# Who makes the low parts of the second block's mixer weights, GpSimd or VectorE

## The reference, cut to what matters

```python
u = rmsnorm(h, mix_norm[l]) @ w_in[l]              # the input matrix: 24 tiles of 128 columns
qa, ka, va, qb, ckv, iq, ik, iw = jnp.split(u, IN_SPLITS_2, axis=-1)
...
o_a = diff_attention(qa, ka, va, lam, bias_a, a_subln[l], lam_init)
...
o_b = dsa_attention(q_lat, c, iq, ik, iw, b_w_uv[l], bias_b, topk)   # keys chosen by top-k of a score
h = h + jnp.concatenate([o_a, o_b], axis=-1) @ w_out[l]              # the output matrix
```

## The kernel before, in words

| piece | stands between | | piece | stands between |
|---|---|---|---|---|
| i0 | the last two sums of the feed-forward before | | i22 | rounds (3,5) and b_inverse 5 |
| i4, i6, i8 | in front of accumulate (0,0) | | o0 | b_mask 11 and b_inverse 10 |
| i10 | accumulate (0,0) and accumulate (0,1) | | o1 | b_top 13 and a_mix 8 |
| i12 | keep 0 and accumulate (1,0) | | o2 | b_top 15 and b_inverse 15 |
| i14 | rounds (1,2) and rounds (1,3) | | o3 | b_y_low 3 and a_y_low 0 |
| i16 | a_bias 3 and accumulate (2,2) | | o4 | a_bias 13 and z_first 1 |
| i18 | rounds (2,5) and a_mix 6 | | o5 | a_bias 14 and z_first 3, a_mix 14, a_bias 15 |
| i20 | accumulate (3,2) and b_inverse 0 | | o6, o7 | a_mix 15 and z_first 5; a_y_low 3 and the final sums |

## Time and profile before

### The profile page before, as it was taken

How to read it: one execution, slowest core, us unless ns; L and a number is a source line. 1 busy time by engine, 2 the same in 40 slices (tenths; PEclk the granted TensorE clock), 3 DMA queues, 4 the chain that set the end, 5 groups by cost and what they waited for, 6 DMA issues and landing times.

```text
span 3181.8 us, 39367 instructions
## 1 busy us (share of the span) xinstructions
PE 3068.4 (96%) x16470; PEld 2560.6 (80%) x16470; DVE 1412.6 (44%) x2112; ACT 1178.7 (37%) x1907; POOL 385.4 (12%) x281
## 2 busy tenths in 40 slices
PE   8999999899999999999989999999999789799999
PEld 7888876788888888886788888899998657688888
DVE  3332455653335333365573333644323666554432
ACT  3322366442314322166543222522223456442321
POOL 0000133200001000024310001200014122120000
PEclk9999999999999999999999999999999799899999
DMA  4223221122232322331122233222233101022232
GB/s 156 93 92 93 95 87 58 62 100 99 90 92 76 109 99 88 98 108 54 67 80 93 93 92 94 75 90 93 83 92 107 34 27 41 34 87 93 96 89 80
DMA packets 76497, 269.62 MB, mean 85 GB/s; under 512 B 8721, under 2 KB 9009, under 8 KB 76065
## 3 DMA queue, kind: packets, MB, share of 16 engines
q1 hardware_dynamic: 74448, 260.08, 25.2%
q0 software_dynamic: 1872, 7.04, 0.7%
HBM read 264.97 MB, written 2.11 MB: 84 GB/s over the span
## 4 chain that ended last, share of the span: by engine, by line
PE 89%; DVE 6%; ACT 4%; issue 1%; POOL 0%; DMA 0%; DVEq 0%; ACTq 0%; POOLq 0%
PE psum L341 25%; PE psum L344 24%; PE psum L347 24%; PE psum L402 3%; PE psum L414 2%; PE psum L360 1%; PE psum L364 1%; PE psum L362 1%; PE psum L638 1%; DVE x_lo L701 1%; PE psum L2591 1%; ACT w_hi L286 1%; DVE b_rank L2866 1%; PE psum L1580 0%; ACT prob L1719 0%
## 5 line engine op out<-in xcount | busy, mean ns | idle before, releaser
L297 DVE TENSOR_TENSOR w_lo<-w_raw,w_hi 128x1024 fp32r<-128x1024 f32 (+1 forms) x436 | 546.7, 1255 | 1250.0 <-ACT w_hi L286 1249.9
L341 PE MATMUL psum<-x_hi,w_hi 128*128 128x512 f32 (+1 forms) x2792 | 968.2, 371 | 8.1 <-ACT neg_mean L2662 5.2
L344 PE MATMUL psum<-x_hi,w_lo 128*128 128x512 f32 (+1 forms) x2792 | 950.6, 365 | 0.0
L347 PE MATMUL psum<-x_lo,w_hi 128*128 128x512 f32 (+1 forms) x2792 | 945.5, 363 | 0.0
L286 ACT CAST w_hi<-w_raw 128x1024 fp32r<-128x1024 f32 (+1 forms) x490 | 504.5, 1030 | 1165.3 <-PE psum L347 1126.5
L341 PEld LDWEIGHTS psum<-x_hi,w_hi 128*128 128x128 f32 x2792 | 502.9, 190 | 114.7 <-issue 17.7
L344 PEld LDWEIGHTS psum<-x_hi,w_lo 128*128 128x128 f32 x2792 | 502.2, 190 | 87.9 <-issue 5.7
L347 PEld LDWEIGHTS psum<-x_lo,w_hi 128*128 128x128 f32 x2792 | 502.2, 190 | 84.0
L341 PE MATMUL psum<-h_hi_ffn,w_hi 128*128 128x512 f32 (+1 forms) x792 | 296.9, 375 | 0.0
L344 PE MATMUL psum<-h_hi_ffn,w_lo 128*128 128x512 f32 (+1 forms) x792 | 292.2, 369 | 0.0
L347 PE MATMUL psum<-h_lo_ffn,w_hi 128*128 128x512 f32 (+1 forms) x792 | 290.7, 367 | 0.0
(11 more groups left out here) (384 smaller groups left out, 3434.2 us busy)
## 6 DMA issues: line engine op xcount, KB each, us to landing
w_raw<-in_ffn_gu SPq DMA_DIRECT2D x176, 512.0 KB, 3.2
w_raw<-in_ffn_down SPq DMA_DIRECT2D x64, 512.0 KB, 3.5
w_raw<-in_w_in SPq DMA_DIRECT2D x44, 512.0 KB, 3.2
w_raw<-in_b_gate SPq DMA_DIRECT2D x44, 512.0 KB, 3.2
w_raw<-in_b_up SPq DMA_DIRECT2D x44, 512.0 KB, 3.2
w_raw<-in_b_down SPq DMA_DIRECT2D x32, 512.0 KB, 3.5
w_raw<-in_ffn_down SPq DMA_DIRECT2D x32, 384.0 KB, 3.1
w_raw<-in_b_in SPq DMA_DIRECT2D x24, 512.0 KB, 3.2
```

The source lines that it names most:

```text
L297: nc.vector.tensor_tensor(w_lo[s][:, 0:n], w_raw[r][:, 0:n], w_hi[s][:, 0:n].bitcast(F32), ALU.subtract).then_inc(*w_low_dve.inc(u))
L341: nc.tensor.matmul(out, w_h, hi[:, c], start=first and i == 0, stop=False)
L344: nc.tensor.matmul(out, w_l, hi[:, c], start=False, stop=False)
L347: done = nc.tensor.matmul(out, w_h, lo[:, c], start=False, stop=final and i == n - 1)
```

## The change

VectorE takes over 19 of the 32 subtractions: i0, the even pieces from i4 to i22, and all of o0 to o7. GpSimd keeps the odd pieces of the input matrix, and i2, since a rule below the changed line gives it pieces 1 to 3 of this stage anyway.

```diff
 def pool_pieces(plan, first):
 
     names = list(first)
-    mine = set(u for u, p in enumerate(plan) if p[0] in ("b2_in", "b2_out"))
+    mine = set(u for u, p in enumerate(plan) if p[0] == "b2_in" and (u - first["b2_mix"]) % 2)
     for name in names:
         if name.startswith("mix_"):
             mine |= set(range(first[name] + WIDE_GROUP + 1, first[name] + IN_TILES_1, 2))
         if name != names[0] and name not in widened(first):
             mine |= set(range(first[name] + 1, first[name] + 4))
```

## The result

| | before | changed |
|---|---|---|
| median of 11 runs | 3183.11 us (3182.76 to 3184.57) | 3190.64 us (3188.62 to 3192.17) |
| ratio, 95% interval | | 1.0024 [1.0016, 1.0031] |
| span of the profiled execution | 3181.8 us | 3189.5 us |
| mean granted clock | 0.985 | 0.983 |

The kernel is 7.5 us slower. That is inside the range on record and on its upper side; it is also just over the 0.2% that the forecast "no difference that counts" allowed. The sum was +3.9 us.

A forecast was written before the change was run, and what follows sets the result against it. TensorE was taken to bound the kernel, with 89% of the chain. The terms 1.23 + 0.1 + 0.5 + 1.23 + 0.85 = +3.9 us on 3183.83 gave 3187.7 us, range 3182 to 3195.5.

The forecast's parts named there:

- no difference that counts: Whole kernel: 3187.7 us, +0.12%, under the 0.2% or 6.4 us that a measurement can tell.
- The sum: Added delays at i12, i14, i16, i18 and o5, together +3.9 us.
- the four named ones: Pieces priced at 0.5 us or more: i12 +1.23, i16 +0.5, i18 +1.23, o5 +0.85 us.
- exposed-waits rival: At i16 the wait is not absorbed and the VectorE-bound 35 us start late: +8.8 us, 3192.6; chance 0.25.
- The sign that the prediction named for it: accumulate (2,3) coming more than 1 us later against a_bias 4 than before would show exposed waits.
- i18 ... +1.23: In VectorE's busy 35 us, ahead of a_bias 7, for which TensorE waits 5.02 us: +1.23 us.
- i12, i16 and o5: Terms ahead of accumulate (1,0), accumulate (2,2) and a_bias 15: +1.23, +0.5 and +0.85 us.
- The lower clock: Longer waits at i12, i18 and o5 draw out the 1.2 GHz share: 3 us more, 3190.7; chance 0.12.
- The test that I wrote for it: A mean clock under 0.79 between 2480 and 2610 us would show the clock case.
- The freed port: VectorE operations stretched beside GpSimd's subtractions get 4.8 us back, additions lie beside waits: 3179.0; chance 0.08.
- the rule as the prediction put it: Two-SBUF-input VectorE operations and SBUF-reading GpSimd operations exclude each other; by it alone, gain of 45 less 23 us.
- Within 0.2%: Whole kernel's time differs by no more than 0.2%: chance 0.64; slower 0.32, faster 0.04.

The follow-up runs named there:

- e3: Kernel before, with VectorE making only i12, i16, i18 and o5: 3189.47 us, ratio 1.0021 [1.0012, 1.0030].
- e4: Kernel before, with VectorE making the other fifteen pieces and GpSimd i12, i16, i18 and o5: 3183.00 us, ratio 1.0001.
- e6: Kernel before, with only piece i16 given to VectorE: 3182.28 us, ratio 0.9997.
- the large filler: Kernel before, with six chained subtractions on VectorE at i18's place, result never read; i18 stays GpSimd's: 3187.09 us, ratio 1.0010.
- e8: Changed kernel, all 19 pieces on VectorE, but i12 placed before accumulate (1,3) and i18 before lat_inverse 0: 3183.67 us, ratio 1.0000.
- e1: Kernel before, with VectorE making only the input-matrix pieces, i0 and the even ones i4 to i22: 3190.16 us, ratio 1.0020.
- e7: Kernel before, with only piece i18 given to VectorE: 3189.83 us, ratio 1.0018.
- e12: Changed kernel, with o_norm 0 moved behind a_mix 7 on VectorE: 3186.21 us, ratio 1.0011.
- e2: Kernel before, with VectorE making only the eight output-matrix pieces: 3182.84 us, ratio 0.9999.
- e11: Kernel before, with o_norm 0 moved behind a_mix 7 on VectorE: 3183.07 us, ratio 0.9999.

## Why the prediction was right where it was, and wrong where it was

- **Where each piece matters.** Right, by e3 and e4: fifteen pieces cost nothing measurable, waits for the cast included (in the changed kernel 2.33 us at i14, and 4.28 us at i20, where 2 to 3 us were forecast), and the loss is in the four named ones. The exposed-waits rival is excluded by e6: the 6.36 us wait at i16 was absorbed, and i16 alone ran in 0.9997 [0.9988, 1.0006] of the time. The sign that the prediction named for it is absent too: accumulate (2,3) starts 2.43 us behind a_bias 4 in both kernels.
- **The delay on TensorE.** About right: 1.14 us of wait at i18 for 1.23 counted, 0.95 at i12 for 1.23, 0.72 at o5 for 0.85. The wait at a_bias 7 was forecast at 6.3 us and is 6.16, the one at a_bias 15 at 4.2 and is 4.05.
- **The term that was mis-sized.** "i18 ... +1.23": measured alone, 6.4 us. The step behind it was that a delay of TensorE costs its own length. Here 1.14 us are the wait, and the other 5.3 us are mostly products at 1.2 GHz in stretches behind it that ran at 2.4 GHz before (4.3 us of them between the index scores and a_bias 15). i12, i16 and o5 seem sized too high: the sum counts 2.6 us for them, and no run shows a cost. i12 alone ran in 1.0001 [0.9992, 1.0010] of the time, i16 alone in 0.9997, the output matrix with o5 in 0.9999 [0.9990, 1.0008]; each interval leaves room for the small term. In the changed kernel a_bias 4 behind i16 starts 1.73 us later than before, no more than the 1.77 us at a_score 0, so the 0.5 us are not there. With the four alone (e3) the wait behind o5 did not grow at all.
- **The lower clock.** This rival named the cause and came within 0.1 us of the time (3190.7), in part by luck: it added 6.9 us to a starting time of 3183.83 us, where 7.5 us came on top of 3183.11. Its reasons were partly wrong too: it gave the clock 3 us on top of the full sum, at i12, i18 and o5. The test that I wrote for it, a mean clock under 0.79 between 2480 and 2610 us, did not answer: it is 0.82 in both kernels, and up to 2600 us it is 0.80 in both. The loss that it missed lies behind that stretch. From 2600 to 2700 us, where the earlier trace rows have a clock of 1.00 over 100 us, the changed kernel shows 0.97:

```profile
2480.00:2610.00 130.00, 96.47 (x459) 70.99 (x461) 87.25 (x211) 59.74 (x131) 11.99 (x6) 0.82 0.09 33
2480.00:2600.00 120.00, 87.82 (x424) 66.30 (x424) 85.36 (x208) 53.11 (x120) 9.64 (x5) 0.80 0.09 31
2600.00:2700.00 100.00, 94.06 (x507) 71.10 (x507) 59.73 (x137) 64.28 (x137) 21.41 (x20) 0.97 0.10 33
```

- **The freed port.** Rightly valued at nothing. The one-column operations of line L2903 all take 0.17 us after the change, where two took 2.28 and 0.66 us before, and the fifteen pieces that leave GpSimd in e4 gain no time that can be measured (1.0001 [0.9993, 1.0010]). Beside i15, which stays with GpSimd, an operation of line L2911 that takes 0.22 us elsewhere still takes 2.40 us. So the stretching was real and off the chain. One reading goes too far: the row of 2.28 us has one tensor as input, and the rule as the prediction put it is about two; only the pair of line L2845 and that operation of L2911 speak for it.
- **The class.** "Within 0.2%" had 0.64; the ratio is 1.0024 and its interval, from 1.0016, does not exclude it. The miss behind it is i18.

**What stays open.** Why the products at 2622 us are slow in the changed kernel, with i18 alone and with the four, and fast with the large filler, though the wait before them is 1.42 us in all. The shifts there are 0.99 us (fast, e8), 2.4, 2.8 and 3.6 us (slow), and 3.8 us (fast). The traces narrow it down. These windows are of the changed kernel, and then of the one with the large filler:

```profile
2591.20:2621.90 30.70, 26.87 (x125) 17.38 (x123) 8.55 (x16) 18.23 (x36) 6.17 (x4) 1.00 0.05 18
2621.92:2628.70 6.78, 6.66 (x18) 4.34 (x19) 2.47 (x7) 3.53 (x7) 0.00 (x0) 0.50 0.01 1
```

```profile
2590.95:2632.00 41.05, 37.06 (x169) 24.33 (x168) 16.21 (x32) 25.77 (x52) 10.35 (x8) 1.00 0.08 26
```

In the changed kernel the clock rises to 2.4 GHz behind a_bias 7 at 2591.2 us and falls again at 2621.9 us, when nearly the whole wait of 1.42 us has just passed; the wait ends 30.8 us after the rise. With the large filler the wait ends 31.3 us after the rise, and the clock stays up. All fourteen profiles fall in line: in the five with slow products (changed, e1, e3, e7, e12) the wait ends 30.4 to 30.9 us after the rise, in the nine others 31.3 us or more. So what goes with the difference is not how long the wait is but when it ends, counted from the clock's own last change, and less than half a microsecond lies between the slow and the fast. No kernel here was made to test that. The Trainium skill ("TensorE: Matmul & The Clock Gate", Part 1) says that the gate's monitor runs free of the kernel, so that the same kernel meets it differently from run to run. The two bands of e12 and this order of the profiles agree with that; the eleven runs of i18 alone, all between 3187.6 and 3190.8 us, do not look like it. What i18 costs is shown; by what rule the clock chooses its low stretches is not.

No version here beats both kernels: e2, e4, e8 and e11 can't be told from the kernel before.

## What to carry to other kernels

Work handed to another engine is priced by what stands behind it on that engine's queue: fifteen of nineteen pieces cost nothing measurable, with waits of up to 6.4 us among the nineteen absorbed, and the one that stood in front of TensorE's wait of 5 us made nearly all the loss. Before such a change is given up, move the exposed steps behind that wait; here moving i18, and i12 with it, brought all of it back. And where TensorE already alternates between 1.2 and 2.4 GHz, allow for a small delay a price of several times its length, and read the clock also in the stretches far behind it.

## What the runs showed of the hardware that was not expected

- By the medians, a delay of 1.14 us in one wait of TensorE cost 6.4 us, one of 2.75 us at the same place 3.9 us, and one of 0.95 us a hundred microseconds earlier nothing that could be measured.
- The same products after the same 1.42 us wait were granted 1.00 or 0.67 of the clock over ten microseconds in which TensorE was always busy. Less than half a microsecond in the time from the clock's last rise to the end of the wait goes with the difference.
- VectorE's subtraction is stretched beside GpSimd as well: i6 in the changed kernel took 1.69 us in place of 1.23 while GpSimd subtracted.
